# Stick-breaking layer of a two-block transformer kernel: query, key and gate products with the weights as the stationary operand, so that they and the outputs come out with features on the partitions

## The chip, the cores and the metric

The kernel runs on one core of a Trainium2 chip. The metric is the device time of one execution in microseconds, the median of several runs; lower is better. Everything is fp32 in memory, one sequence of 256 rows, width 2048.

## The reference

Two blocks follow each other. The second block has two layers: one with indexed sparse attention, then the stick-breaking layer that is changed here. Each layer ends in a layer norm and a gated per-layer embedding. The part that matters:

```python
def _stick_breaking_mixer(x, k, v, w_q, w_out):
    q, g = _split(x @ w_q, (ATTN_W, ATTN_W))                  # gate g, queries q: 16 heads of 128
    def block(args):                                          # blocks of 128 query rows
        i, qb = args
        t = i * B_BLOCK + jnp.arange(B_BLOCK)
        z = jnp.einsum('bqhd,bshd->bhqs', qb, k) * scale
        strict = (key_pos[None, :] < t[:, None])[None, None]
        log_keep = jnp.where(strict, jax.nn.log_sigmoid(-z), 0.0)
        between = lax.cumsum(log_keep, axis=3, reverse=True) - log_keep
        a = jnp.where(strict, jnp.exp(jax.nn.log_sigmoid(z) + between), 0.0)
        o = jnp.einsum('bhqs,bshd->bqhd', a.astype(v.dtype), v)
        return o.reshape(B, B_BLOCK, ATTN_W)
    ...
    return (o * jax.nn.silu(g)) @ w_out

kb, vb = _split(x @ w_kv_b, (ATTN_W, ATTN_W))                 # in second_block, before that mixer
x = _layer_norm(DN_ALPHA * x + y, ln_g[i], ln_b[i])           # behind each mixer
x = x + (p[i] @ w_ple[i]) * jax.nn.sigmoid(x @ w_ple_gate[i])
```

So each of the 16 heads has queries q, keys k and values v of 256 rows by 128; scores z, a reverse running sum of their logarithms along the keys, an exponential, the product with v, the gate, and the output product. x is what the layer before left.

## The kernel before

**One stream of weights.** All weights lie packed in the order of use. A block of it is a *slot*: 128 partitions by 1024 values, two of the sixteen tiles of the contraction by 512 output columns. There are 800 slots, counted from 1 here. SyncE loads them into five raw buffers. ScalarE rounds a slot to fp32r (`whi`, line 1164), VectorE takes the difference (`wlo`, line 1511), and PE multiplies with three products instead of one: hi rows by hi weights, hi by lo, lo by hi (lines 849, 850, 851; the rows are `XH` and `XL`). There are three pairs of whi and wlo, so ScalarE may round slot n only when PE has done slot n - 3. PE takes a slot in twelve matmuls, with 128 columns of the rows as the stationary operand and 512 columns of weights moving; the result is 128 rows by 512 features in one PSUM bank for each half of the 256 rows, after eight slots. Such a product over all sixteen tiles is called a run here (`bq1` is the second run of queries); banks G0 to G3 serve runs in pairs, in turn.

**The layer.** Its slots are 606 to 733, in four groups c = 0 to 3 of four heads: runs bg (gate), bq, bk, bv, eight slots each; the output product ob follows from 734. ScalarE moves finished runs out of PSUM (`move_rows`, line 1221): bg through SiLU into `Gd`, bv into `Va`, bq and bk into a row buffer `nat`. Queries and keys are needed with features on the partitions, so the jobs `bq0` to `bk3` (kind "copy") turn each in 8 transposes on PE (line 860), and ScalarE and VectorE copy one bank each into `qTa` and `kTa`.

**The attention of a group** is the job st0 to st3, cut in steps: 0 scores on PE (line 911); 1 mask on VectorE, absolute value on ScalarE; 2 Exp; 3 Ln and a Relu; 4, 5, 6 running sums and subtraction on VectorE (lines 1818 and 1820), one for each third of the scores, with a Relu on ScalarE in 4 and 5; 7 Exp (line 1350); 8 the twelve tiles of weights turned on PE and copied out; 9 weights times values (line 953); 10 times gate on VectorE, line 1832; 11 the result turned back, 8 transposes, and copied into `FT`, from where jobs r4 split it into XH and XL for the output product.

**What sets the order.** A walk over the slots gives every engine its program: before slot s, the rounding and the difference of slot s + 2 (`takes`); the slot; the steps that the table BEHIND names for it; then, if a run ends, the `move` of it; then those of AFTER. Each engine executes its part in this order and waits on semaphores: `half_done` and `slot_done` from PE, `moved` of a bank from whoever emptied it, `hi_done` and `lo_done` for the weights. BEHIND has bq0.0 at slot 622, bk0.0 at 630, st0 from 638 to 650, st1 at 670 (step 0), 671 (1, 2), 672 (3), 673 (4), 675 (5), 676 (6), 678 (7), 679 (8), 680 (9), 681 (10, 11); st2 is 32 slots later, st3 runs from 730 to 743. ScalarE loads a table before a function that the loaded one does not hold; those loads are instructions of its queue.

## Time and profile before

| | us |
|---|---|
| median of 3 runs (2360.76 to 2361.06) | 2360.78 |
| profiled execution, its time | 2361.13 |
| its span, first to last instruction | 2359.8 |
| PE busy | 2345.6 |
| VectorE busy | 1466.2 |
| ScalarE busy | 1146.1 |
| window of the layer's first four groups, slots 606 to 733 | 383.37 |

The window is 1776.95 to 2160.32 us from the start of the span. The busy time of PE is a union of records whose ends are modelled; for its pace the distance from start to start is the thing to read. A record's duration of 0.39 us for a matmul that is followed by the next after 0.23 us is such an overlap. On ScalarE and VectorE, too, the next instruction may begin up to 0.1 us before the end of the last. DVE in a row is VectorE, ACT is ScalarE, PEld the loading of the stationary operand. A wait in a row of the timeline stands in brackets: how long the engine was idle before it and what released it.

### The profile page before, as it was taken

Reading aid. Unit: us, or ns where it says so; the run is one execution under the profiler, and the core shown is the slowest. Engines: PE = TensorE matmul, PEld = TensorE weight load, DVE = VectorE, ACT = ScalarE, POOL = GpSimd, SP = SyncE. Lnnn points to the kernel's source line nnn. Section 1 sums busy time; section 2 is a strip of 40 time slices with the busy share of each in tenths; the row PEclk is TensorE's granted clock in tenths of the full one; section 3 lists DMA queues with packets and bytes.
Section 4 is the critical chain, followed back from the end, with each engine's and each line's share of the span. In section 5 each row is a group of like instructions: output and inputs, shape, how many; then the busy total and the mean of one; then the engine's idle time right before and its main releaser. Section 6 shows DMA issues by size and latency. Waiting matters only on the chain.

```text
span 2359.8 us, 28659 instructions
## 1 busy us (share of the span) xinstructions
PE 2345.6 (99%) x11224; PEld 1956.8 (83%) x11224; DVE 1466.2 (62%) x2045; ACT 1146.1 (49%) x1483; POOL 39.6 (2%) x60
## 2 busy tenths in 40 slices
PE   9999999999999999999999999999999999999999
PEld 5688898988889888888888878888788888888877
DVE  7888765555546455776756775666765455456575
ACT  4344554544445554443344445454545556456453
POOL 0000000000000000000000000000200000000020
PEclk9999999999999999999999999999999999999999
DMA  9986643555554457887655655455665555555565
GB/s 396 396 308 206 198 148 117 178 173 189 190 167 140 142 176 254 293 289 248 214 193 185 196 180 168 153 170 187 229 209 188 176 180 169 179 168 172 198 221 177
DMA packets 131240, 478.97 MB, mean 203 GB/s; under 512 B 15281, under 2 KB 15537, under 8 KB 125985
## 3 DMA queue, kind: packets, MB, share of 16 engines
q1 hardware_dynamic: 126080, 458.41, 58.0%
q0 software_dynamic: 3728, 17.76, 2.0%
q8 instruction: 89, 1.46, 0.3%
q10 hardware_dynamic: 1298, 0.97, 0.1%
q14 instruction: 45, 0.37, 0.0%
HBM read 470.80 MB, written 6.29 MB: 202 GB/s over the span
## 4 chain that ended last, share of the span: by engine, by line
PE 94%; DVE 2%; DMA 2%; ACT 1%; issue 1%; SPq 0%; ACTq 0%; DVEq 0%
PE G L849 26%; PE G L851 26%; PE G L850 26%; PE A L860 4%; DMA ada<-in_weights 2%; PE A L849 2%; PE A L850 2%; PE A L851 2%; PE A L953 1%; PE G L845 1%; PE A L1025 1%; PE A L1008 1%; PE A L911 1%; DVE ada L1525 1%; DVE wlo L1511 1%
## 5 line engine op out<-in xcount | busy, mean ns | idle before, releaser
L1511 DVE TENSOR_TENSOR wlo<-raw,whi 128x1024 fp32r<-128x1024 f32 (+3 forms) x781 | 920.8, 1183 | 696.8 <-ACT whi L1164 694.6
L1164 ACT ACTIVATE whi<-raw 128x1024 fp32r<-128x1024 f32 (+3 forms) x781 | 800.4, 1026 | 823.3 <-PE G L851 735.3
L849 PE MATMUL G<-whi,XH 128*128 128x512 f32 (+3 forms) x2804 | 1081.0, 386 | 2.8 <-DVE wlo L1511 2.3
L851 PE MATMUL G<-whi,XL 128*128 128x512 f32 (+3 forms) x2804 | 1066.9, 381 | 0.0
L850 PE MATMUL G<-wlo,XH 128*128 128x512 f32 (+3 forms) x2804 | 1066.0, 380 | 0.0
L849 PEld LDWEIGHTS G<-whi,XH 128*128 128x128 f32 x2804 | 526.7, 188 | 100.3 <-DVE wlo L1511 7.0
L851 PEld LDWEIGHTS G<-whi,XL 128*128 128x128 f32 x2804 | 526.3, 188 | 94.4
L850 PEld LDWEIGHTS G<-wlo,XH 128*128 128x128 f32 x2804 | 526.9, 188 | 90.4 <-issue 0.2
L849 PE MATMUL A<-whi,XH 128*128 128x512 f32 x192 | 77.4, 403 | 1.6 <-DVE wlo L1511 1.6
L1525 DVE CUSTOM_DVE_ANT_0 ada<-ada,dil 128x2048 f32<-128x2048 f32 x32 | 75.1, 2347 | 5.3 <-DMA ada<-in_weights 5.3
L850 PE MATMUL A<-wlo,XH 128*128 128x512 f32 x192 | 74.8, 390 | 0.0
L851 PE MATMUL A<-whi,XL 128*128 128x512 f32 x192 | 74.8, 389 | 0.0
L1221 ACT ACTIVATE nat<-G 128x512 f32<-128x512 f32 (+3 forms) x98 | 54.1, 569 | 29.3 <-PE G L851 29.1
L1221 ACT ACTIVATE dil<-G 128x512 f32<-128x512 f32 x64 | 36.8, 597 | 24.6 <-PE G L851 24.5
L849 PEld LDWEIGHTS A<-whi,XH 128*128 128x128 f32 x192 | 36.0, 188 | 12.6 <-issue 2.7
L1543 DVE SCALAR_TENSOR_TENSOR accg<-raw,small,accg 128x512 f32<-128x512 f32 x60 | 44.9, 748 | 1.1
L850 PEld LDWEIGHTS A<-wlo,XH 128*128 128x128 f32 x192 | 36.1, 188 | 8.4 <-issue 1.2
L851 PEld LDWEIGHTS A<-whi,XL 128*128 128x128 f32 x192 | 36.0, 188 | 7.6
L860 PE MATMUL A<-ident,nat 128*128 128x128 f32 x306 | 41.0, 273 | 0.5 <-ACT PT__91 L1295 0.5
L860 PEld LDWEIGHTS A<-ident,nat 128*128 128x128 f32 x306 | 35.8, 140 | 6.5 <-issue 0.9
L1288 ACT ACTIVATE dil<-A 128x512 f32<-128x512 f32 x25 | 14.9, 597 | 49.2 <-PE A L860 49.2
L1300 ACT ACTIVATE FT<-A 128x512 f32<-128x512 f32 x12 | 7.2, 597 | 51.8 <-PE A L860 51.8
(235 smaller groups left out, 1516.0 us busy)
## 6 DMA issues: line engine op xcount, KB each, us to landing
raw<-in_weights SPq DMA_DIRECT2D x724, 512.0 KB, 3.8
ada<-in_weights SPq DMA_DIRECT2D x32, 1024.0 KB, 11.2
raw<-in_weights SPq DMA_DIRECT2D x80, 384.0 KB, 3.2
raw<-in_weights SPq DMA_DIRECT2D x16, 288.0 KB, 2.9
spill<-nat POOLq DMA_DIRECT2D x8, 512.0 KB, 5.4
CP<-spill POOLq DMA_DIRECT2D x8, 512.0 KB, 6.3
raw<-in_weights SPq DMA_DIRECT2D x8, 336.0 KB, 3.5
FT<-in_xT SPq DMA_DIRECT2D x4, 512.0 KB, 5.8
```

The lines of the kernel that those rows point to most:

```text
L845: ins = pe.matmul(acc, whole_operand(name)[:, k, half], raw[o.home[n]][:, w], start=(k == start), stop=(k == end - 1))
L849: pe.matmul(acc, xh[:, k, half], wh, start=(k == start), stop=False)
L850: pe.matmul(acc, xh[:, k, half], wl, start=False, stop=False)
L851: ins = pe.matmul(acc, xl[:, k, half], wh, start=False, stop=(k == end - 1))
L860: ins = pe.transpose(P[bank][0:a.shape[1], 128 * n:128 * n + 128], a, ident[:, :])
L911: ins = pe.matmul(P[bank][:, x:x + nk], l, r, start=(n == 0), stop=(n == len(ps) - 1))
L953: ins = pe.matmul(P[A0 + qb][:, h * 128:(h + 1) * 128], PT[:, n * 128:(n + 1) * 128], v(h, kb), start=(kb == 0), stop=(kb == qb))
L1164: ac.activation(whi[r % NSPL][:, 0:2 * cols], raw[o.home[n]][:, 0:2 * cols], ACT.Copy).then_inc(hi_done, 1)
L1221: ac.activation(dst[:, hf, 0:cols], P[bank][:, 0:cols], func).then_inc(moved[bank], 1)
L1511: ve.tensor_tensor(wlo[r % NSPL][:, 0:2 * cols], raw[o.home[n]][:, 0:2 * cols], whi[r % NSPL][:, 0:2 * cols].bitcast(F32), ALU.subtract).t ...
L1525: ve.tensor_tensor_reduce(b, b, cs, 1.0, cols_[:, f:f + 1], ALU.mult, ALU.add, mods[:, f:f + 1]).then_inc(modulated, 1)
L1543: ins = ve.scalar_tensor_tensor(out=dst, in0=b, scalar=cc, in1=dst, op0=ALU.mult, op1=ALU.add)
```

## The change

The products bg, bq and bk of the layer take the weights as the stationary operand and the rows as the moving one, so the result has features on the partitions.

- Each of these twelve runs becomes two, `a` and `b`, of 256 output columns (two heads) and four slots. A slot now holds four contraction tiles by 256 columns. The count of slots stays 800.
- XH and XL become the two halves of one tensor `XHL`, tile by tile, so that one matmul moves 512 columns, XH and XL of a tile, past a tile of whi; a second moves XH alone, 256 columns, past wlo. A slot is sixteen matmuls (`turned_slot`): two heads by four contraction tiles by two. The bank then holds hi and lo parts side by side.
- When a run ends, VectorE adds the two parts of each head with a reduction (`TENSOR_REDUCE`, 128x512 to 128x256) directly into its place in `qTa`, `kTa` or the gate. For bg, ScalarE then applies SiLU in place, waiting for both reductions. ScalarE no longer moves bg, bq and bk out of PSUM.
- The jobs bq and bk (transposes and copies) are gone. Step 9 multiplies the values, as stationary operand, with the turned weights, 4 matmuls of 256 and 4 of 128 columns in fp32; the outputs come out turned. Step 10 multiplies by the turned gate and writes FT; step 11 is gone.
- In group 0, bv0 is placed ahead of bg0; in the other groups the order stays.

```diff
+    def plan_turned(w, c0):
+        for half in range(2):
+            plan.extend(("w", w, c0 + 256 * half, 512, k) for k in range(0, KT, 4))
+
     for c in range(4):
-        plan_gemm([("w_qb", 2048 + 512 * c, 512, KT), ("w_qb", 512 * c, 512, KT),
-                   ("w_kvb", 512 * c, 512, KT), ("w_kvb", 2048 + 512 * c, 512, KT)])
+        if c == 0:
+            plan_gemm([("w_kvb", 2048, 512, KT)])
+        plan_turned("w_qb_t", 2048 + 512 * c)
+        plan_turned("w_qb_t", 512 * c)
+        plan_turned("w_kvb_t", 512 * c)
+        if c:
+            plan_gemm([("w_kvb", 2048 + 512 * c, 512, KT)])
...
-        return {0: (A0, A1, A3), 8: (A2, A1, A3), 9: (A0, A1), 11: (A2, A3)}.get(step, ())
+        return {0: (A0, A1, A3), 8: (A2, A1, A3), 9: (A0, A1)}.get(step, ())
...
-        for x in "gqkv":
-            whole_run(f"b{x}{c}")
+        if c == 0:
+            whole_run("bv0")
+        for x in "gqk":
+            for half in "ab":
+                run(f"b{x}{c}{half}", 512, "T")
+                slots.extend((f"b{x}{c}{half}", k) for k in range(0, KT, 4))
+        if c:
+            whole_run(f"bv{c}")
...
-    XH = sb("XH", 53376, [128, KT, T], F32R)
-    XL = sb("XL", 69760, [128, KT, T], F32R)
+    XHL = sb("XHL", 53376, [128, KT, 2, T], F32R)
+    XH, XL = XHL[:, :, 0, :], XHL[:, :, 1, :]
...
+    GT = [g.rearrange("p q n -> p (q n)").rearrange("p (h t) -> p h t", h=4) for g in Gd]
...
+    def turned_place(name):
+
+        dst = {"q": qTa, "k": kTa, "g": GT[int(name[2]) % 2]}[name[1]]
+        return dst[:, 0:2, :] if name[3] == "a" else dst[:, 2:4, :]
...
-            elif name in ("om0", "oa0", "bg0", "ob0"):
-                job = {"om0": "r1", "oa0": "r2", "bg0": "r3", "ob0": "r4"}[name]
+            elif name in ("om0", "oa0", "bv0", "ob0"):
+                job = {"om0": "r1", "oa0": "r2", "bv0": "r3", "ob0": "r4"}[name]
...
+        def turned_slot(s):
+
+            name, k0 = slots[s]
+            if k0 == 0:
+                for bank, nth in use[name]:
+                    pe.wait_ge(moved[bank], nth - 1)
+            pe.wait_ge(lo_done, o.rank[s] + 1)
+            wh, wl = whi[o.rank[s] % NSPL], wlo[o.rank[s] % NSPL]
+            for h in range(2):
+                acc = P[use[name][h][0]]
+                for kk in range(4):
+                    k = k0 + kk
+                    w = slice(256 * kk + 128 * h, 256 * kk + 128 * h + 128)
+                    both = XHL[:, k, :, :].rearrange("p s t -> p (s t)")
+                    if k < KT - 1:
+                        pe.matmul(acc[:, :], wh[:, w], both, start=(k == 0), stop=False)
+                        ins = pe.matmul(acc[:, 0:T], wl[:, w], XH[:, k, :], start=False, stop=False)
+                    else:
+                        pe.matmul(acc[:, 0:T], wl[:, w], XH[:, k, :], start=False, stop=False)
+                        ins = pe.matmul(acc[:, :], wh[:, w], both, start=False, stop=True)
+                if h == 0 and k0 + 4 == KT:
+                    ins.then_inc(half_done, 1)
+            ins.then_inc(slot_done, 1)
...
-                weighted_values(job, step, PT2, lambda h, kb: Va[:, kb, h * 128:(h + 1) * 128])
-            elif step == 11:
-                heads_turned(job, step, S2, 9)
+                for bank, nth, _ in fill[(job, 8)]:
+                    pe.wait_ge(moved[bank], nth)
+                for bank, nth, _ in fill[(job, 9)]:
+                    pe.wait_ge(moved[bank], nth - 1)
+                for h in range(4):
+                    acc = P[(A0, A1)[h // 2]][:, h % 2 * T:h % 2 * T + T]
+                    v = [Va[:, kb, h * 128:(h + 1) * 128] for kb in range(2)]
+                    pe.matmul(acc, v[0], PT2[:, 384 * h:384 * h + 256], start=True, stop=False)
+                    ins = pe.matmul(acc[:, 128:256], v[1], PT2[:, 384 * h + 256:384 * h + 384], start=False, stop=True)
+                    if h % 2:
+                        ins.then_inc(side_full, 1)
...
-            elif name in ("bg2", "bg3"):
-                bank, nth, _ = fill[(f"st{int(name[2]) - 2}", 9)][1]
-                ac.wait_ge(moved[bank], nth)
...
-            elif name[:2] in ("ag", "bg"):
+            elif name[:2] == "ag":
                 gate_room(name)
                 move_rows(name, Gd[int(name[2]) % 2], ACT.Silu)
+            elif name[:2] == "bg":
+                for bank, nth in use[name]:
+                    ac.wait_ge(moved[bank], nth)
+                ac.activation(turned_place(name), turned_place(name), ACT.Silu).then_inc(gate_made, 1)
...
+            elif name[:2] in ("bg", "bq", "bk"):
+                turned_room(name)
+                for h in range(2):
+                    product_done(name, h)
+                    bank = use[name][h][0]
+                    ve.tensor_reduce(turned_place(name)[:, h, :], P[bank][:, :].rearrange("p (s t) -> p t s", s=2),
+                                     AX, ALU.add).then_inc(moved[bank], 1)
...
+        def turned_room(name):
+
+            c = int(name[2])
+            if name[1] != "g":
+                ve.wait_ge(side_full, fill[(f"st{c - 1}" if c else "att3", 0)][2][2])
+            elif c == 0:
+                ve.wait_ge(ple_added, 8)
+            else:
+                for bank, nth, _ in fill[(f"st{c - 2}", 9) if c > 1 else ("att3", 5)]:
+                    ve.wait_ge(moved[bank], nth)
...
-                rows = S2[:, 0:1024].rearrange("p (q n) -> p q n", q=2)
-                for bank, nth in use[f"bg{c}"]:
-                    ve.wait_ge(moved[bank], nth)
-                for qb in range(2):
-                    bank, nth, no = fill[(job, 9)][qb]
+                ve.wait_ge(gate_made, 2 * c + 2)
+                for n in range(2):
+                    bank, nth, no = fill[(job, 9)][n]
                     ve.wait_ge(side_full, no)
-                    ve.tensor_tensor(rows[:, qb, :], P[bank][:, :], Gd[c % 2][:, qb, :], ALU.mult).then_inc(moved[bank], 1)
-            elif step == 11:
-                heads_moved(job, step, 4 * c)
+                    ve.tensor_tensor(FT[:, 4 * c + 2 * n:4 * c + 2 * n + 2, :], P[bank][:, :].rearrange("p (h t) -> p h t", h=2),
+                                     GT[c % 2][:, 2 * n:2 * n + 2, :], ALU.mult).then_inc(moved[bank], 1)
```

Three places where the order of instructions moves. First PE in bk3: the end of its first slot (718), the turning of bq3 and the start of the next slot (nat is the row buffer, ident the identity; A is one of the banks A0 to A3, G one of G0 to G3). Before:

```order
L851 MATMUL G<-whi_56,XL 128x512
L849 MATMUL G<-whi_56,XH 128x512
L850 MATMUL G<-wlo_59,XH 128x512
L851 MATMUL G<-whi_56,XL 128x512
L860 MATMUL A<-ident,nat_70 128x128 x8
L849 MATMUL G<-whi_54,XH 128x512
L850 MATMUL G<-wlo_57,XH 128x512
L851 MATMUL G<-whi_54,XL 128x512
```

After, PE in a turned slot of the same group, in bq3a (in these rows the moving operand is named first):

```order
L906 MATMUL G<-XHL,whi_54 128x512
L907 MATMUL G<-XHL,wlo_57 128x256
L906 MATMUL G<-XHL,whi_54 128x512
L907 MATMUL G<-XHL,wlo_57 128x256
L906 MATMUL G<-XHL,whi_54 128x512
L907 MATMUL G<-XHL,wlo_57 128x256
```

The transposes are gone there, and matmuls of 512 and 256 columns alternate.

Second, VectorE beside st1, from the difference for slot 675 (wlo_58) on; L1818 are the four running sums of step 4 (TENSOR_TENSOR_SCAN in the trace), L1820 their subtraction. Before:

```order
L1511 TENSOR_TENSOR wlo_58<-raw_51,whi_55 128x1024
L1818 SCALAR_TENSOR_TENSOR CP<-dil,CP 128x128 x4
L1820 TENSOR_TENSOR dil<-dil,CP 128x512
L1511 TENSOR_TENSOR wlo_59<-raw_52,whi_56 128x1024
L1511 TENSOR_TENSOR wlo_57<-raw_53,whi_54 128x1024
L1818 SCALAR_TENSOR_TENSOR CP<-dil,CP 128x256 x2
L1820 TENSOR_TENSOR dil<-dil,CP 128x512
```

After, where L1905 and L1907 are the same two lines and L1725 the two reductions of bg2a:

```order
L1580 TENSOR_TENSOR wlo_58<-raw_51,whi_55 128x1024
L1905 SCALAR_TENSOR_TENSOR CP<-dil,CP 128x128 x4
L1907 TENSOR_TENSOR dil<-dil,CP 128x512
L1725 TENSOR_REDUCE dil<-G 128x256 x2
L1580 TENSOR_TENSOR wlo_59<-raw_52,whi_56 128x1024
L1580 TENSOR_TENSOR wlo_57<-raw_53,whi_54 128x1024
L1905 SCALAR_TENSOR_TENSOR CP<-dil,CP 128x256 x2
```

The reductions stand between the subtraction and the differences for slots 676 and 677.

Third, ScalarE at the same place; L1344 is the Ln of step 3, L1345 and L1347 Relu, whi_56 and whi_54 the rounding of slots 676 and 677. Before:

```order
L1344 ACT_TABLE_LOAD
L1344 ACTIVATE dil<-dil,ones 128x512 x3
L1345 ACTIVATE CP<-dil 128x512
L1164 ACTIVATE whi_55<-raw_51 128x1024
L1347 ACTIVATE CP<-dil 128x512
L1164 ACTIVATE whi_56<-raw_52 128x1024
L1164 ACTIVATE whi_54<-raw_53 128x1024
L1347 ACTIVATE CP<-dil 128x512
L1164 ACTIVATE whi_55<-raw_49 128x1024
L1164 ACTIVATE whi_56<-raw_50 128x1024
L1221 ACT_TABLE_LOAD
L1221 ACTIVATE dil<-G 128x512 x2
```

After, with L1415, L1416 and L1418 for those lines and L1331 the SiLU of bg2a, then of bg2b:

```order
L1415 ACT_TABLE_LOAD
L1415 ACTIVATE dil<-dil,ones 128x512 x3
L1416 ACTIVATE CP<-dil 128x512
L1239 ACTIVATE whi_55<-raw_51 128x1024
L1418 ACTIVATE CP<-dil 128x512
L1331 ACT_TABLE_LOAD
L1331 ACTIVATE dil<-dil 128x512
L1239 ACTIVATE whi_56<-raw_52 128x1024
L1239 ACTIVATE whi_54<-raw_53 128x1024
L1418 ACTIVATE CP<-dil 128x512
L1239 ACTIVATE whi_55<-raw_49 128x1024
L1239 ACTIVATE whi_56<-raw_50 128x1024
```

The SiLU and its table load stand ahead of the rounding of slots 676 and 677; before, they stood behind the rounding of 679.

## Rows read from the trace of the kernel before

**Rows 1.** the page: busy time of PE (section 1), the chain by engine (section 4)
```profile
PE 2345.6 (99%) x11224; PEld 1956.8 (83%) x11224; DVE 1466.2 (62%) x2045; ACT 1146.1 (49%) x1483; POOL 39.6 (2%) x60
...
PE 94%; DVE 2%; DMA 2%; ACT 1%; issue 1%; SPq 0%; ACTq 0%; DVEq 0%
```

**Rows 2.** windows, slots 638 to 669: length; busy PE, PEld, DVE, ACT, POOL; clock; DMA
```profile
1866.70:1963.42 96.72, 96.72 (x461) 80.86 (x460) 50.15 (x52) 53.77 (x62) 0.00 (x0) 1.00 0.54 174
```

**Rows 3.** timeline of PE: start, duration; fp32r matmuls of 288 and 512 columns
```profile
243.77 0.29 PE L850 MATMUL G<-wlo,XH 128*128 128x288 f32 x1
...
244.83 0.29 PE L849 MATMUL G<-whi,XH 128*128 128x288 f32 x1
...
1988.46 0.39 PE L849 MATMUL G<-whi,XH 128*128 128x512 f32 x1
...
1991.18 0.39 PE L849 MATMUL G<-whi,XH 128*128 128x512 f32 x1
```

**Rows 4.** timeline of PE: slots 622 and 623, with the turning of bq0
```profile
1821.36 0.39 PE L849 MATMUL G<-whi,XH 128*128 128x512 f32 x1
...
1824.09 1.04 PE L860 MATMUL A<-ident,nat 128*128 128x128 f32 x8
1824.88 0.47 PE L849 MATMUL G<-whi,XH 128*128 128x512 f32 x1
...
1827.73 0.39 PE L849 MATMUL G<-whi,XH 128*128 128x512 f32 x1
```

**Rows 5.** timeline of PE: scores of st0, then its values and turned outputs
```profile
1869.42 2.78 PE L911 MATMUL A<-dil 128*128 128x128 f32 x16
1871.86 0.58 PE L849 MATMUL G<-whi,XH 128*128 128x512 f32 x1
...
1903.62 2.84 PE L953 MATMUL A<-dil,CP 128*128 128x128 f32 x24
1906.21 0.48 PE L849 MATMUL G<-whi,XH 128*128 128x512 f32 x1
...
1909.83 0.48 PE L849 MATMUL G<-whi,XH 128*128 128x512 f32 x1
...
1912.64 0.39 PE L849 MATMUL G<-whi,XH 128*128 128x512 f32 x1
```

**Rows 6.** groups by line and shape: reductions on VectorE; busy us, mean ns
```profile
L1770 DVE TENSOR_REDUCE st__92<-S__90 128x1 f32<-128x768 f32 x8 | 7.5, 942 | 0.0
...
L1769 DVE TENSOR_REDUCE st__92<-S__90 128x1 f32<-128x384 f32 x8 | 4.4, 553 | 0.3
```

**Rows 7.** timeline of ScalarE beside st1: start, duration, idle before
```profile
1973.71 1.28 ACT L1344 ACT_TABLE_LOAD   x1
...
1977.38 1.05 ACT L1164 ACTIVATE whi<-raw 128x1024 fp32r<-128x1024 f32 x1
1978.33 0.62 ACT L1347 ACTIVATE CP<-dil 128x512 f32<-128x512 f32 x1
1978.85 2.12 ACT L1164 ACTIVATE whi<-raw 128x1024 fp32r<-128x1024 f32 x2
...
1991.98 1.49 ACT L1350 ACTIVATE dil<-dil 128x1536 f32<-128x1536 f32 x1
```

**Rows 8.** timeline of VectorE beside st1
```profile
1978.46 1.23 DVE L1511 TENSOR_TENSOR wlo<-raw,whi 128x1024 fp32r<-128x1024 f32 x1 [3.51 <-ACT whi L1164]
1979.60 1.36 DVE L1818 TENSOR_TENSOR_SCAN CP<-dil,CP 128x128 f32<-128x128 f32 x4
1981.00 0.69 DVE L1820 TENSOR_TENSOR dil<-dil,CP 128x512 f32<-128x512 f32 x1
1981.61 2.35 DVE L1511 TENSOR_TENSOR wlo<-raw,whi 128x1024 fp32r<-128x1024 f32 x2
```

**Rows 9.** timeline of PE: first matmuls of slots 675 and 676
```profile
1979.74 0.50 PE L849 MATMUL G<-whi,XH 128*128 128x512 f32 x1
...
1982.88 0.50 PE L849 MATMUL G<-whi,XH 128*128 128x512 f32 x1
```

65 lines of the change are left out of this document (37 added, 28 removed), and 13 rows, old and new, of the table BEHIND.

## The prediction

> **What bounds the kernel now.** The page comes first. Matmuls fill 2345.6 of the 2359.8 us, and 94% of the chain of waits is on PE [rows 1], so a saving counts only if it takes time out of PE's own row of work, and a wait counts only if PE meets it. The windows by stretch say the same of the layer that is changed: its second group of heads, from 1866.70 to 1963.42, has PE busy in all 96.72 us at a granted clock of 1.00, while VectorE works 50.15 and ScalarE 53.77 us [rows 2]. Both look half idle. But every slot of weights passes through both in turn (the rounding on ScalarE, line 1164, then the difference on VectorE, line 1511), only three slots of room ahead of PE, and both engines take their instructions in a fixed order. So the timelines of ScalarE and VectorE beside the attention steps must be read, not their busy shares.
>
> A slot is twelve matmuls of 512 columns. From its first start to that of the next slot lie 2.72 us (1988.46 to 1991.18), 0.227 a matmul. With 288 columns eight steps take 1.06 us (243.77 to 244.83), 0.133 each [rows 3]. The durations in the rows (0.39 and 0.29) overlap; only starts count here.
>
> **What leaves PE.** (1) The turning of query and key rows: 8 transposes behind one slot for each of the eight tiles bq and bk. The slot that starts at 1821.36 is followed at 1824.88, 3.52 us on where 2.72 would be undisturbed, and the next slot takes 2.85 until 1827.73 [rows 4]. That is 0.80 + 0.13, about 0.9 us for each of eight: 7.3 us. (2) The turning of the outputs, step 11 of the four st jobs: the same 8 transposes, slots at 1906.21, 1909.83 and 1912.64 [rows 5]. 3.62 + 2.81 against 5.44 is 1.0, of which about 0.1 belongs to the step before: 0.9 each, 3.7 us in all. (3) Weights times values: 24 records of 128 columns take 2.59 us (1903.62 to 1906.21 [rows 5]). Now there are 8 of 256 and 8 of 128, the shape of today's scores, whose 16 records take 2.44 (1869.42 to 1871.86 [rows 5]): 0.15 less, 0.5 us over four. Sum: -11.5 us. The ScalarE and VectorE copies that go with (1) and (2) are off the path and give nothing by themselves. Twenty-four ScalarE moves out of PSUM also go; that frees ScalarE where it already waits for PE.
>
> **What comes onto PE.** The 96 slots of bg, bq and bk keep their 6144 columns but spread them over sixteen matmuls: eight of 512 and eight of 256, each with its own weight load. No fp32r matmul of 256 columns is in the trace. A line through the two steps of [rows 3] (0.227 at 512, 0.133 at 288, so 0.42 ns a column and 12 ns a matmul) gives 0.120 us at 256. A slot then takes 8 x 0.227 + 8 x 0.120 = 2.775 us, 0.053 more: +5.1 us over 96. The bounds: below, 0.108 us, the step of the 24 records of values, each with its load (2.59 / 24 [rows 5]); above, the 0.133 of the 288 columns, which would hold if the load and not the columns set that step. Over 768 short matmuls that is -9 to +10 us. I take 0.120 because 288 columns, the nearest row, still follow the line. The Trainium skill, TensorE: Matmul & The Clock Gate, section Back-to-back issue gap, gives columns / 2.4 + 2.5 ns for a matmul; by it the extra four matmuls would cost 0.01 us a slot, 1 us in all instead of 5, but it also gives 216 ns for 512 columns where this trace has 227, so the rows stand.
>
> **What is moved: the reductions and the gate.** Every turned tile now ends with two reductions on VectorE (hi part plus lo part, 128x512 from PSUM to 128x256). The reductions in the trace take 553 ns for 384 elements and 942 for 768 [rows 6], 1.0 ns an element, so 0.68 us for 512; the next instruction starts about 0.08 earlier, so 0.60 each. For bq and bk that hides: rounding and difference (1.06 and 1.23 us [rows 7, 8]) have two slots of 2.72 to be done in, so 1.2 us of reductions fit into what is left. For the gate it does not, because ScalarE's SiLU, which used to read PSUM on its own, now waits in ScalarE's queue for VectorE's second reduction, and the rounding of the next slots stands behind it. And bg is now two tiles of four slots, so the first gate tile ends at slot 673, in the middle of the scans of st1, where before the only gate move came at slot 677.
>
> I work st1 through on the clock of before. VectorE: the difference for slot 675 starts at 1978.46, four scans at 1979.60, their subtraction at 1981.00, and it is free at 1981.61 [rows 8]. There the differences for slots 676 and 677 stand now, and PE starts slot 676 at 1982.88 [rows 9]. In the changed order the two reductions come first: free at 1982.8, result out at 1982.9. ScalarE has been waiting for that since 1978.9; before it had rounded slot 676 from 1978.85 on [rows 7]. Now the table load for SiLU (1.28 us, as the one at 1973.71 [rows 7]), 0.5 us of SiLU (a ScalarE step of 512 at 1978.33 hands on after 0.52 [rows 7]), and the rounding of 676 starts at 1984.7 instead of 1978.85. Rounding to difference is 1.1 us (1977.38 to 1978.46), the difference 1.23: slot 676 can start at 1987.1. PE starts slot 675 at 1979.74 [rows 9] and is through at 1982.5. **PE waits about 4.4 us.** Behind that the two other scan steps of st1 are late too: difference 676, 677, scans and subtraction of step 5 (1.9), difference 678, step 6 (1.9), difference 679, the two reductions of the second gate tile, at 1995.4; then SiLU (0.5), a rounding (0.95), the table load for Exp (1.28) and the Exp (1.49 [rows 7]) end at 1999.9, while PE stands before step 8 from 1998.2: 1.7 us more. So st1 costs 6.1, where the same slots lose 0.64 today (0.42 of it at 1982.88 [rows 9] and the rest as small waits at slots 674 and 676). Net +5.4. The steps of st2 stand at the same slots relative to theirs: +5.4. For st0 the first gate tile ends one slot earlier in its scans (slot 641, with step 4 at 642), so the reductions run before the scans and only table load and SiLU delay the rounding, by 1.9 us, of which slack takes some: 1.6 us; the second gate tile comes behind step 6 and holds the rounding of 648 until PE has lost 1.8 more. 3.4 against 0.3 today: +3.1. st3 has no gate tile beside it: 0. Sum of new waits: +13.9 us. Bounds: if a reduction takes 0.55 instead of 0.68 the waits are 1.4 us less, at 0.9 (a strided read of PSUM, which no row shows) 2 us more.
>
> bv0 moves ahead of bg0; it waits for the same x_lo counts, and its values now lie ready early. One more wait is new on PE, that step 0 waits for reductions in place of copies; for st0 the last of them ends about 0.9 us behind slot 637 and PE has slot 638 in between, so nothing.
>
> **The sum.** -11.5 + 5.1 + 13.9 = +7.5 us. The chains above pass some ten times from engine to engine, which I took at nothing and which costs about 0.05 us each time (1977.38 + 1.05 against 1978.46 [rows 7, 8]): +8.0 us. The profiled execution has a span of 2359.8 [rows 1] and a time of 2361.13, so it becomes 2367.8 and 2369.1; its time is 0.35 above the median of 2360.78, and the forecast for the median is 2368.8 us, 0.34% slower. A measurement of this kernel can tell about 0.2% (4.7 us) from no change.
>
> **Rivals.**
> *The gate queue doesn't bind (faster).* If the table load is over before the reductions end, or ScalarE and VectorE run ahead further than I have them because their copies are gone, the waits stay what they are and -11.5 + 5.1 = -6.4: 2354.4 us. For it: both engines are half idle [rows 2]. Against: the wait comes from order, not load, and the slack of slot 676 is 1.7 us (its rounding starts at 1978.85, with 2.4 of work, for a use at 1982.88 [rows 7, 9]). The rival holds if the rounding of 676 starts before about 1980.5 on this clock. Chance 0.13, with half of it spread between this and no change.
> *The short matmul is bound by its weight load.* 0.133 us instead of 0.120, +10 us, of which the waits give 3 back: 2376. For it: each matmul has its load and none so short is in the trace. Against: 288 columns and the 128-column transposes [rows 3, 4]. Chance 0.11.
> *A 256-column fp32r matmul runs at the fp32 rate.* The scores' rows [rows 5] are 8 of 256 and 8 of 128 columns in 2.44 us, about 0.2 us for each of 256: 768 x 0.09 = +70 us, 2438. Nothing in the trace speaks for it. Chance 0.02.
> *PE's clock falls in the pause.* The granted clock is 1.00 in all of the layer [rows 2], but PE is busy in all of it, and here two pauses of over 4 us come. At 1.2 GHz a turned slot takes twice its 2.78 us; one slot at that level in each of two places is +5.6 us, less what the later wait of 1.7 takes back: about 2373. The Trainium skill, TensorE: Matmul & The Clock Gate, section Part 1: The HAM clock gate, says that an idle engine falls to half its clock; no run here shows at what pause. Chance 0.10.
>
> **How the numbers follow.** The forecast has 0.62, with its own range from 2363 (short matmul near its lower bound) to 2375 (slower reductions). The rest is as above, 0.02 unnamed. To hold 8 in 10 the range reaches to the clock case and over most of the load case and part of the way to the faster one: 2358 to 2379. Slower by over 0.2% (above 2365.5): 0.52 of the forecast, 0.10, 0.11 and 0.02 make 0.75. Faster (below 2356.1): 0.09 of the first rival and 0.01. Within: the remaining 0.15.
>
> **What would show it.** In the changed trace: no transposes of nat beside bq and bk, and none behind the values; turned slots 2.775 us apart, eight starts 0.120 and eight 0.227 us; reductions of 0.68 us; a ScalarE table load before each first gate SiLU that waited for VectorE; PE waiting for the difference (line 1511's successor) once for over 4 us in each of the second and third groups, at the third slot behind the first gate tile, and for the Exp before step 8; for 1 to 2 us twice in the first. The window of the second group should be 96.7 - 2.9 + 1.3 + 3.1 = 98.2 us, that of the third some 2.3 longer. I am wrong if the layer's slots are 2.72 or over 2.83 us, or if the rounding of the third slot doesn't stand behind the SiLU.

## The result, and the profile after

The changed kernel takes 2375.44 us (median of 4 runs, 2374.29 to 2376.70), the kernel before 2360.92 beside it (4 runs, 2360.76 to 2362.83): slower by 0.6%, ratio 1.006 [1.0042, 1.0077]. The forecast was 2368.8, range 2358 to 2379. The sign, the place and the main mechanism came as written. The time is 6.6 us above the forecast, though. For the profiled execution, forecast at 2369.1, it is 5.2: the turned slots are slower by 4.3 than forecast, two more terms that were off by nearly 4 each, TensorE's clock and the waits, cancel, and the time outside the span adds 1.4, less 0.7 that was gained ahead of the layer.

The profiled execution took 2374.29 us with a span of 2371.6 (before 2361.13 and 2359.8 [rows 1]): +11.8 in the span and 1.4 outside it. The page, sections 1 and 4, which answer to [rows 1]:

```profile
PE 2346.3 (99%) x11480; PEld 1968.2 (83%) x11480; DVE 1487.1 (63%) x2081; ACT 1131.2 (48%) x1455; POOL 39.6 (2%) x60
...
PE 92%; DVE 3%; DMA 2%; ACT 2%; issue 1%; SPq 0%; ACTq 0%; DVEq 0%
```

PE is hardly busier than before (2346.3 against 2345.6), so what left it and what came onto it, slots at a lower clock included, nearly cancel. The span grew by what PE stood still, and VectorE and ScalarE together have 2 points more of the chain. The windows by stretch say where: the kernel before first (slots 614 to 637, 670 to 701, 702 to 729, 730 to 765; 638 to 669 is [rows 2]), then the changed kernel (the same stretches, with 638 to 669 second). The columns are those of [rows 2]; the clock is third from the end.

```profile
1799.60:1866.70 67.10, 67.10 (x305) 55.72 (x304) 30.79 (x26) 30.32 (x34) 0.00 (x0) 1.00 0.58 188
1963.42:2060.54 97.12, 96.99 (x462) 80.77 (x460) 50.23 (x52) 52.48 (x61) 0.00 (x0) 1.00 0.53 173
2060.54:2146.81 86.27, 86.14 (x413) 71.77 (x412) 47.10 (x51) 49.21 (x59) 0.00 (x0) 1.00 0.52 170
2146.81:2250.87 104.06, 103.42 (x481) 85.86 (x480) 62.33 (x70) 52.86 (x60) 0.53 (x1) 1.00 0.57 188
```

```profile
1798.88:1866.71 67.83, 67.83 (x385) 58.84 (x384) 35.56 (x35) 28.16 (x28) 0.00 (x0) 1.00 0.55 186
1866.71:1965.97 99.26, 96.57 (x526) 82.82 (x524) 56.18 (x63) 49.61 (x54) 0.00 (x0) 1.00 0.51 170
1965.97:2067.93 101.96, 97.72 (x525) 84.12 (x524) 55.63 (x61) 48.70 (x54) 0.00 (x0) 0.98 0.47 165
2067.93:2159.59 91.66, 87.42 (x477) 75.66 (x476) 52.57 (x60) 45.44 (x52) 0.00 (x0) 0.96 0.46 160
...
2159.59:2262.67 103.08, 102.44 (x465) 84.80 (x464) 61.63 (x69) 52.38 (x59) 0.53 (x1) 1.00 0.56 190
```

The five differences are +0.73, +2.54, +4.84, +5.39 and -0.98 us, +12.5 together (the first 605 slots happened to be 0.7 quicker). The second stretch holds the scans of st0, the third those of st1, the fourth those of st2; where the forecast and the expectations speak of waits in the first, second and third group, these are meant. The stretches with st0 and st1 were forecast at 98.2 and 100.5 us and are 99.26 and 101.96. Those with st1 and st2 lose most, and they alone show a clock below 1.00.

**The queue behind the gate.** ScalarE beside st1, the place of [rows 7]; then VectorE, the place of [rows 8]; then PE at slots 676 and 677 and at 708 and 709, the place of [rows 9]:

```profile
1980.96 0.62 ACT L1418 ACTIVATE CP<-dil 128x512 f32<-128x512 f32 x1
1985.60 1.28 ACT L1331 ACT_TABLE_LOAD   x1 [4.02 <-DVE dil L1725]
1986.89 0.63 ACT L1331 ACTIVATE dil<-dil 128x512 f32<-128x512 f32 x1
1987.43 1.99 ACT L1239 ACTIVATE whi<-raw 128x1024 fp32r<-128x1024 f32 x2
```

```profile
1981.09 1.23 DVE L1580 TENSOR_TENSOR wlo<-raw,whi 128x1024 fp32r<-128x1024 f32 x1 [3.51 <-ACT whi L1239]
1982.23 1.36 DVE L1905 TENSOR_TENSOR_SCAN CP<-dil,CP 128x128 f32<-128x128 f32 x4
1983.63 0.69 DVE L1907 TENSOR_TENSOR dil<-dil,CP 128x512 f32<-128x512 f32 x1
1984.24 1.28 DVE L1725 TENSOR_REDUCE dil<-G 128x256 f32<-128x512 f32 x2
1988.50 2.36 DVE L1580 TENSOR_TENSOR wlo<-raw,whi 128x1024 fp32r<-128x1024 f32 x2 [2.98 <-ACT whi L1239]
```

```profile
1989.78 0.50 PE L906 MATMUL G<-XHL,whi 128*128 128x512 f32 x1 [4.24 <-DVE wlo L1580]
...
1994.24 0.39 PE L906 MATMUL G<-XHL,whi 128*128 128x512 f32 x1
...
2091.75 0.80 PE L906 MATMUL G<-XHL,whi 128*128 128x512 f32 x1 [4.24 <-DVE wlo L1580]
...
2096.78 0.40 PE L906 MATMUL G<-XHL,whi 128*128 128x512 f32 x1
```

Read them as one chain. ScalarE is done with its Relu at 1981.6 and stands for 4.02 us before the gate's SiLU, because VectorE has a difference, four scans and a subtraction to do before the two reductions. These end at 1985.5, and only then do the table load, the SiLU and the rounding follow (1987.43), the difference (1988.50), and PE, which had slot 675 done 4.24 us earlier. Slot 676 then takes 4.46 us (1989.78 to 1994.24) and slot 708 takes 5.03, where an undisturbed turned slot takes 2.83. The granted clock over them, from the windows:

```profile
1989.78:1994.24 4.46, 4.46 (x17) 3.83 (x18) 4.43 (x6) 1.10 (x2) 0.00 (x0) 0.62 0.67 229
2091.75:2096.78 5.03, 5.03 (x17) 4.31 (x17) 5.00 (x7) 1.10 (x2) 0.00 (x0) 0.53 0.59 208
```

TensorE was at its lower level, 1.2 GHz, for most of both: that cost 1.6 and 2.2 us at these two slots. Beside st0 PE waits 1.15 and 1.50 us (idle times ahead of its first matmuls at 1887.44 and 1900.81), and the clock stays up.

**The turned slots.** PE's timeline, starts of one slot in the quicker and one in the slower rhythm that they show:

```profile
1874.93 0.39 PE L906 MATMUL G<-XHL,whi 128*128 128x512 f32 x1
...
1877.70 0.39 PE L906 MATMUL G<-XHL,whi 128*128 128x512 f32 x1
...
1927.23 0.40 PE L906 MATMUL G<-XHL,whi 128*128 128x512 f32 x1
1927.47 0.28 PE L907 MATMUL G<-XHL,wlo 128*128 128x256 f32 x1
1927.58 0.40 PE L906 MATMUL G<-XHL,whi 128*128 128x512 f32 x1
...
1930.07 0.40 PE L906 MATMUL G<-XHL,whi 128*128 128x512 f32 x1
```

2.77 us from slot start to slot start in the first, as forecast; 2.83 in the second, and that is the usual one: of the 96 turned slots only some ten, behind a step 0 or a step 9, are quick. In the turned slots of the trace a long matmul is followed by a short one after 0.235 us (median) and a short one by a long one after 0.117.

### The profile page after: what moved, and what is told of

It is laid out like the page before. It is cut to its first block, busy times and chain, and to the rows that moved or that the text cites. A ratio compares the mean times of both kernels' runs of the same rounds, so it can differ in the third digit from the quotient of the medians.

```text
span 2371.6 us, 29207 instructions
## 1 busy us (share of the span) xinstructions
PE 2346.3 (99%) x11480; PEld 1968.2 (83%) x11480; DVE 1487.1 (63%) x2081; ACT 1131.2 (48%) x1455; POOL 39.6 (2%) x60
## 4 chain that ended last, share of the span: by engine, by line
PE 92%; DVE 3%; DMA 2%; ACT 2%; issue 1%; SPq 0%; ACTq 0%; DVEq 0%
PE G L884 23%; PE G L886 23%; PE G L885 23%; PE G L906 6%; PE A L919 3%; PE G L907 3%; DMA ada<-in_weights 2%; PE A L884 2%; PE A L885 2%; PE A L886 2%; PE G L880 1%; PE A L1018 1%; DVE wlo L1580 1%; PE A L1098 1%; PE A L1081 1%
## 5 line engine op out<-in xcount | busy, mean ns | idle before, releaser
L884 PE MATMUL G<-whi,XHL 128*128 128x512 f32 (+3 forms) x2420 | 928.9, 384 | 2.2 <-DVE wlo L1580 2.0
L886 PE MATMUL G<-whi,XHL 128*128 128x512 f32 (+3 forms) x2420 | 917.3, 379 | 0.0
L885 PE MATMUL G<-wlo,XHL 128*128 128x512 f32 (+3 forms) x2420 | 916.6, 379 | 0.0
L884 PEld LDWEIGHTS G<-whi,XHL 128*128 128x128 f32 x2420 | 454.6, 188 | 83.2 <-DVE wlo L1580 4.4
L886 PEld LDWEIGHTS G<-whi,XHL 128*128 128x128 f32 x2420 | 454.3, 188 | 79.4
L885 PEld LDWEIGHTS G<-wlo,XHL 128*128 128x128 f32 x2420 | 454.9, 188 | 76.0 <-issue 0.2
L906 PE MATMUL G<-XHL,whi 128*128 128x512 f32 x720 | 261.1, 404 | 11.2 <-DVE wlo L1580 11.1
L907 PE MATMUL G<-XHL,wlo 128*128 128x256 f32 x720 | 203.5, 283 | 0.0
L906 PEld LDWEIGHTS G<-XHL,whi 128*128 128x128 f32 x720 | 137.1, 190 | 43.8 <-DVE wlo L1580 12.8
L907 PEld LDWEIGHTS G<-XHL,wlo 128*128 128x128 f32 x720 | 137.8, 191 | 2.3
L884 PE MATMUL A<-whi,XHL 128*128 128x512 f32 x192 | 77.2, 402 | 1.6 <-DVE wlo L1580 1.6
L885 PE MATMUL A<-wlo,XHL 128*128 128x512 f32 x192 | 74.8, 389 | 0.0
L886 PE MATMUL A<-whi,XHL 128*128 128x512 f32 x192 | 74.7, 389 | 0.0
L884 PEld LDWEIGHTS A<-whi,XHL 128*128 128x128 f32 x192 | 36.1, 188 | 11.8 <-issue 2.7
```

What stands on the lines that cost most here:

```text
L884: pe.matmul(acc, xh[:, k, half], wh, start=(k == start), stop=False)
L885: pe.matmul(acc, xh[:, k, half], wl, start=False, stop=False)
L886: ins = pe.matmul(acc, xl[:, k, half], wh, start=False, stop=(k == end - 1))
L906: pe.matmul(acc[:, :], wh[:, w], both, start=(k == 0), stop=False)
L907: ins = pe.matmul(acc[:, 0:T], wl[:, w], XH[:, k, :], start=False, stop=False)
```

## The experiments

All times are medians. The kernel before took 2360.6 to 2360.8 us beside every one of them.

**The SiLU out of the scans.**

```diff
-            elif name[:2] == "bg":
-                for bank, nth in use[name]:
-                    ac.wait_ge(moved[bank], nth)
-                ac.activation(turned_place(name), turned_place(name), ACT.Silu).then_inc(gate_made, 1)
+            elif name[:2] == "bk" and name[3] == "b":
+                for gate in (f"bg{name[2]}a", f"bg{name[2]}b"):
+                    for bank, nth in use[gate]:
+                        ac.wait_ge(moved[bank], nth)
+                    ac.activation(turned_place(gate), turned_place(gate), ACT.Silu).then_inc(gate_made, 1)
```

> The changed kernel with the two gate SiLUs of each group taken out of the scans and done behind the last key tile of the group. Theory (ScalarE's queue stands behind the gate's reduction): the rounding for slot 676 runs at once, only the 1.2 us of reductions still stand before its difference, so PE waits 1.3 us there instead of 4.4, the same in the third group, the waits of the first group (1.3, 1.7 and some tenths) go, and TensorE's clock stays at 1.00, which gives back 1.7 and 2.2 us: 2375.4 - 6.2 - 3.5 - 3.9 = about 2362. Rival (VectorE's reductions make the wait, and the queue only adds the 1.9 us of table load and SiLU to it): PE still waits over 2 us in each group, about 2369. Rival (the time is in the slots, not in the waits): within 1 us of the changed kernel.

Measured: 2364.22 us, ratio to before 1.0015 [1.0006, 1.0024]; clock 1.00 in every stretch of the layer. Moving two short instructions on an engine that is half idle gives 11.2 of the 14.5 us back. The wait behind slot 675 is 1.5 us (1.3 expected), so the theory holds and both rivals fall. By the profiled spans (2371.6 and 2362.2) the gain is 9.4 us, though, where the theory has 13.6. Of what is missing, 3.5 us stand in waits that were in no trace so far: 1.24 us each at slots 674 and 706, 1.04 at slot 735.

**The reduction out of the scans too.** In the walk, behind the slot and ahead of its steps:

```diff
+            late = self.slots[s - 2]
+            if late[0][:2] == "bg" and late[0][3] == "a" and late[1] == 12:
+                self.walk.append(("move", late[0], 0))
```

> As the kernel with the late SiLUs, and the reductions of each group's first gate tile two slots later, behind the difference for slot 677. Theory: no new wait is left beside the scans; what remains of the change is 11.5 us of PE work removed and 96 slots of 2.83 in place of 2.72 us (+10.3): 2360.9 - 11.5 + 10.3 = about 2359.7, and clock 1.00. If the reductions cost the same wherever they stand (rival): as the kernel with the late SiLUs alone, about 2362.

Measured: 2363.00 us, 1.001 [1.0, 1.002], against 2359.7 expected. The wait behind slot 675 is down to 0.3 us as expected, but the new waits at 674, 706 and 735 stay, and the stretch with st0 is now 0.9 us longer (96.68 against 95.77 us by the windows): there the reduction had been in a free place. ScalarE's timeline beside step 2 of st1 in this kernel shows where the new wait comes from:

```profile
1971.94 1.28 ACT L1416 ACT_TABLE_LOAD   x1
1973.23 1.67 ACT L1416 ACTIVATE dil<-dil 128x512 f32<-128x512 f32 x3
```

The groups of ScalarE's instructions by line count the loads ahead of this Exp, first in the kernel before (line 1340), then in this one:

```profile
L1340 ACT ACT_TABLE_LOAD x1 | 1.3, 1283 | 0.0
```

```profile
L1416 ACT ACT_TABLE_LOAD x4 | 5.1, 1283 | 0.1
```

One in the whole layer before, one in each group now. With the SiLU behind bk the last Exp's table is gone when step 2 comes, and the 1.28 us fall into ScalarE's busiest stretch. In the kernel before, and in the changed one, SiLU stood between Ln and Exp. It took a load of its own there too, but the Exp behind it needed one in any case. The traces count 41 loads in each of these two kernels, 44 with the late SiLUs, and 37 where a copy stands in place of SiLU (below).

**The table loaded early.** `bg1a` is reduced in its old place, and behind the late SiLUs:

```diff
+                ac.activation(spare[:, 0:1], ident[:, 0:1], ACT.Exp)
```

> As the kernel with both late, with two mends: the first gate tile of the first group is reduced where it was (there the later place cost 0.9 us: 96.67 against 95.77 us for that group), and behind the two late SiLUs stands an Exp of one column, so that ScalarE loads the table for Exp where it has time. Theory (the new waits of the late kernels, 1.24 us at slots 674 and 706 and 1.04 us at slot 735, are one more table load of 1.28 us that came to stand at step 2 of the scans): 2363.0 - 0.9 - 2.5 - 1.0 = about 2358.6, and slot 674 takes 2.81 us. Rival (the load hides in any place, the waits come from something else): 2362.

Measured: 2358.18 us, 0.9989 [0.998, 0.9998]. The waits at 674, 706 and 735 are gone (slot 674 takes 2.81 us, slot 735 3.41 as in the kernel before), and all of PE's time beside the scans is work. The windows, slots 614 to 729 in four stretches:

```profile
1799.59:1867.42 67.83, 67.83 (x386) 58.84 (x384) 35.68 (x35) 27.43 (x27) 0.00 (x0) 1.00 0.57 187
1867.42:1963.19 95.77, 95.77 (x525) 82.82 (x524) 56.08 (x63) 52.08 (x59) 0.00 (x0) 1.00 0.55 176
1963.19:2059.36 96.17, 96.17 (x525) 82.91 (x524) 55.47 (x61) 50.35 (x56) 0.00 (x0) 1.00 0.55 175
2059.36:2144.68 85.32, 85.32 (x477) 73.92 (x476) 52.14 (x60) 47.07 (x54) 0.00 (x0) 1.00 0.53 169
```

So the change as such is a small gain (about 2.5 us), which its queue order, with all that followed from it, had buried under 17.

**Query and key alone.** Gate, values and outputs as in the kernel before, with step 11 back in its places:

```diff
-        for x in "gqk":
+        whole_run(f"bg{c}")
+        for x in "qk":
             for half in "ab":
```

> One part of the change alone: query and key products turned, gate, values and the turning of the outputs as in the kernel before. Theory (only the gate's turning makes PE wait): -7.3 us for the 64 transposes and their trailing slots, +7.0 for 64 slots of 2.83 in place of 2.72, reductions of query and key hidden: 2360.8 - 0.3 = about 2360.5, with waits beside the scans as in the kernel before and clock 1.00. Rival (the reductions on VectorE or the slots of four tiles cost beside the scans by themselves): over 2363.

Measured: 2359.59 us, 0.9995 [0.9986, 1.0004]; clock 1.00, and no wait of PE that the kernel before does not have. The reductions of query and key cost nothing beside the scans; the whole loss comes with the rest of the change, and the kernels above put it on the gate.

**The pause filled.** Twelve matmuls that read only XHL, behind slots 675 and 707:

```diff
             ins.then_inc(slot_done, 1)
+            if s + 1 in (675, 707):
+                for _ in range(12):
+                    pe.matmul(acc[:, :], XH[:, 0, 0:128], both, start=False, stop=False)
```

> The changed kernel with twelve more matmuls of 512 columns (2.7 us) put on PE at the start of the pause of 4.4 us behind slots 675 and 707; they add to the gate's sums, so the output is not the reference's. Nothing else moves. Theory (the clock falls because PE stands still for over 4 us): the pauses are 1.7 us, the granted clock stays 1.00 behind them, the slots behind them take 2.8 instead of 4.5 and 5.0 us; the waits before step 8 of up to 1.7 us, which the slow slots hid, come back in part: 1 to 4 us less than the changed kernel, 2371.5 to 2374.5. Rival (the fall has another cause, such as the power of the short matmuls): the clock falls at the same places and the time stays within 1 us.

Measured: 2372.74 us, 1.0051 [1.0036, 1.0066], clock 1.000 in all four runs where the changed kernel had 0.996 to 0.998. PE's waits beside st1, and the window behind the first:

```profile
1989.70 0.50 PE L906 MATMUL G<-XHL,whi 128*128 128x512 f32 x1 [1.50 <-DVE wlo L1583]
...
2002.59 1.53 PE L922 MATMUL A<-ident,dil 128*128 128x128 f32 x12 [1.43 <-ACT dil L1424]
```

```profile
1989.70:1993.00 3.30, 3.30 (x19) 2.89 (x20) 3.27 (x5) 1.22 (x3) 0.00 (x0) 1.00 0.70 214
```

The same time passes, but PE is at work in it, and the clock stays. This shows that the pause makes the clock fall. It also shows the second wait of the forecast, the one before step 8 (1.7 us forecast, 1.43 here), which the changed kernel doesn't have: there the slow slots give the scans the time. So the clock's fall costs 3.8 us where it happens and much less in the end. In the profiled executions the stretch with st1 takes 101.96 us with the pause filled and without, and the one with st2 91.11 in place of 91.66: 0.6 us in all, because slots 679 and 711, behind which the wait stands, take 5.65 and 5.62 us to the next slot in place of 4.13 and 4.06. The median spans (2372.7 and 2371.1) differ by 1.6 and the median times by 2.7; what differs between the executions of the changed kernel is open. The low level does not last equally long in all: in the profiled one with the banks in turn (below), slot 676 took 5.12 us.

**A copy in place of SiLU.** One word, `ACT.Copy` for `ACT.Silu`; no table load in the chain.

> The changed kernel with a plain copy in place of the gate's SiLU, in the same place of ScalarE's order: no table load before it (1.28 us). The gate is left without its SiLU, so the output is not the reference's. Theory (reductions, table load and SiLU stand one behind the other ahead of the rounding): the pauses behind slots 675 and 707 shrink by the load alone, from 4.24 to 2.96 us, that in the first group from 1.15 to about 0, and TensorE's clock does not fall behind them, while the waits before step 8 grow to some 1.4 us as they did with the pause filled: 2375.4 - 2.6 - 1.1 - 3.9 + 2.6 = about 2370.4. Rival (a pause of 3 us is enough for the clock to fall): about 2372. Rival (the load is over before the reductions are): no change.

Measured: 2369.71 us, 1.0037 [1.0023, 1.0051]. The pauses and the clock of the slots behind them:

```profile
1986.80 0.80 PE L906 MATMUL G<-XHL,whi 128*128 128x512 f32 x1 [2.96 <-DVE wlo L1580]
...
2088.60 0.80 PE L906 MATMUL G<-XHL,whi 128*128 128x512 f32 x1 [2.96 <-DVE wlo L1580]
```

```profile
1986.80:1992.09 5.29, 5.29 (x16) 4.51 (x17) 5.25 (x7) 1.11 (x2) 0.00 (x0) 0.50 0.64 205
2088.60:2092.95 4.35, 4.35 (x16) 3.73 (x17) 4.32 (x6) 1.10 (x2) 0.00 (x0) 0.63 0.69 210
```

4.24 - 2.96 = 1.28 us, the table load to the hundredth: it is in the chain and nothing hides it. The Trainium skill, ScalarE: Activation LUTs, section What ACT_TABLE_LOAD costs, adds a drain of about 1.38 us to each load; here the measurement decides, and there is none: the SiLU starts at 1986.89, where the load that began at 1985.60 ends. The 2370.4 was near for a wrong reason, though: the clock was to stay up, and it fell after 2.96 us too. By the two profiled spans the kernel gains 3.7 us, 2.6 in the pauses and 1.4 in the stretch with st0 (97.83 against 99.26), while the slow slots cost 0.5 more (5.29 and 3.12 at slots 676 and 677 and 4.35 at slot 708, in place of 4.46, 2.81 and 5.03) and hide the wait before step 8 as they did. The median gains 5.7, since the other runs of the changed kernel have spans of 0.7 to 1.9 us more than its profiled one.

**The order of PE's matmuls.** Three orders of the same sixteen. Grouped, on the changed kernel:

```diff
-                for kk in range(4):
+                last = k0 + 4 == KT
+                for kk, long in [(kk, long) for long in ((False, True) if last else (True, False)) for kk in range(4)]:
```

Banks in turn, on the changed kernel: `for kk in range(4) for h in range(2)` in all slots but a tile's last. And, on the kernel with the early table, one order in all slots; in the changed kernel the last k-tile of a half has its short matmul ahead of its long one:

```diff
-                    if k < KT - 1:
...
-                    else:
-                        pe.matmul(acc[:, 0:T], wl[:, w], XH[:, k, :], start=False, stop=False)
-                        ins = pe.matmul(acc[:, :], wh[:, w], both, start=False, stop=True)
+                    pe.matmul(acc[:, :], wh[:, w], both, start=(k == 0), stop=False)
+                    ins = pe.matmul(acc[:, 0:T], wl[:, w], XH[:, k, :], start=False, stop=(k == KT - 1))
```

> The changed kernel with the matmuls of each half slot in another order: four of 512 columns, then four of 256 (the last slot of a tile the other way round), instead of in turn. The measured slot is 2.83 us, where eight steps of 0.227 and eight of 0.120 would be 2.775. Theory (the surplus of 0.055 comes from the alternation of long and short): slot 2.775, about 5 us less than the changed kernel, 2370. Rival (a short matmul behind a short one is bound by its weight load, 0.133 us): slot 2.88, about 5 us more, 2380. Rival (the surplus belongs to sixteen matmuls in whatever order): 2.83 and no change.

Measured: 2373.81 us, so neither the 2370 of the theory nor the 2380 of the first rival; a turned slot takes 2.80, and the first 24 take 67.32 us instead of 67.83. Short behind short starts after 0.119 us (median), so the load rival is out and the short step is the 0.120 of the line through [rows 3]. Long behind long starts after 0.234, where [rows 3] has 0.227. The surplus is in the long ones.

> The changed kernel with the two PSUM banks of a turned tile filled in turn, a pair of matmuls each, instead of eight matmuls into one and then eight into the other (the last slot of a tile stays as it is). What the grouped order showed: the short step is 0.120 us as worked out, the long one 0.234 instead of 0.227. Theory (a long matmul pays 7 ns because it adds to the bank that the one ahead of it wrote): turned slots of 2.775 us, 4 us less than the changed kernel, about 2371.5. Rival (the bank has nothing to do with it): 2.83, no change, 2375.4.

Measured: 2373.87 us (2372.56 to 2375.26); turned slots 2.83 as in the changed kernel, and the steps are the same 0.235 and 0.117. So the slots don't depend on the bank; the theory falls. The 1.6 us between the medians are not in the slots, and the times of two of the four runs (2375.06 and 2375.26) lie among those of the changed kernel.

> As the kernel with the table loaded early, but the last k-tile of a turned half keeps the order of all others (512 columns, then 256); there it was the other way round, so two long and two short matmuls stood side by side. In the traces so far a turned slot takes 2.773 us behind the scores or values of a step and 2.83 from the next tile's first slot on. Theory (the turned-round pair at a tile's end takes PE out of the quicker rhythm): the slots behind each step 0 and step 9 stay at 2.77 until the next disturbance, so up to 2 us less, 2356.5. Rival (the rhythm has another cause): no change, 2358.2.

Measured: 2356.53 us, 0.998 [0.9971, 0.9989]. From step 0 of st0 on the undisturbed turned slots take 2.77 us, all but 709 to 711, behind a short wait, with 2.83. One of group 1 by its starts:

```profile
1918.02 0.39 PE L910 MATMUL G<-XHL,whi 128*128 128x512 f32 x1
1918.25 0.28 PE L911 MATMUL G<-XHL,wlo 128*128 128x256 f32 x1
1918.37 0.39 PE L910 MATMUL G<-XHL,whi 128*128 128x512 f32 x1
...
1920.79 0.39 PE L910 MATMUL G<-XHL,whi 128*128 128x512 f32 x1
```

The 24 slots ahead of step 0 still take 67.83 us. A long matmul is followed after 0.236 us there (median) and after 0.230 in a quick slot. So the odd pair at a tile's end takes PE out of the quick rhythm, but it is not the only thing that does, and something in the attention steps brings PE in.

> As the grouped kernel with late SiLUs, but every slot has its four long matmuls ahead of its four short ones, in the last slot of a tile too. Theory as above (the turned-round order at a tile's end sets the rhythm): turned slots of 2.78 in place of 2.805 us, up to 2 us less, 2355. Rival: no change, 2356.9.

Measured: 2357.01 us (2356.91 in the grouped order with the odd tile end, below): no change, 2.80 as before. The theory falls here: grouped slots have one rhythm, between the two.

The grouped order on the kernel with the early table:

> As the kernel with the table loaded early, with the grouped order of matmuls in the turned slots as well. Theory: the two gains add, since one is in waits and the other in PE's own steps (24 undisturbed turned slots took 67.33 instead of 67.83 us, 0.02 each): 2358.6 - 2.0 = about 2356.6, under the kernel before by 0.18%. Rival (shorter slots let PE reach the same waits earlier, and they take it back): 2358.6.

Measured: 2356.91 us, 0.9984 [0.9975, 0.9992]: 1.3 of the 2.0 us.

```diff
+            if s + 1 == 614:
+                for _ in range(4):
+                    pe.matmul(P[use[name][0][0]][:, 0:128], ident[:, :], ident[:, :], start=True, stop=True)
```

> As the kernel with one order in all turned slots, with four fp32 products of the identity with itself (128 columns) put on PE ahead of the first turned slot, 614; their sums are overwritten by the tile's first matmul. The 24 turned slots ahead of the first attention step still took 2.83 us there, all behind it 2.77. Theory (any few short fp32 matmuls ahead of a turned tile put PE into the quicker rhythm, which then lasts): these 24 take 2.773, so 1.37 us less and 0.45 for the four, 2356.5 - 0.9 = 2355.6, and the stretch of slots 614 to 637 takes 67.0 instead of 67.83 us. Rival (the rhythm comes from something else in the attention steps, such as the wait for another engine): the stretch takes 67.83 + 0.45 = 68.3 us, 2357.0.

Measured: 2355.86 us, 0.9978 [0.9969, 0.9987], the lowest median of all and 0.22% under the kernel before. The slots behind the four are at 2.77 us until the scores of st0; the slots 640 to 648 behind these scores are at 2.83, where they were at 2.77 without the four (starts of PE, slots 622 and 623 and then 641 and 642, and the window from slot 614 to the scores of st0, ahead of it that of the kernel without the four):

```profile
1821.56 0.39 PE L913 MATMUL G<-XHL,whi 128*128 128x512 f32 x1
...
1824.34 0.39 PE L913 MATMUL G<-XHL,whi 128*128 128x512 f32 x1
...
1876.98 0.40 PE L913 MATMUL G<-XHL,whi 128*128 128x512 f32 x1
...
1879.81 0.40 PE L913 MATMUL G<-XHL,whi 128*128 128x512 f32 x1
```

```profile
1799.21:1869.86 70.65, 70.65 (x401) 61.31 (x400) 36.61 (x36) 30.22 (x31) 0.00 (x0) 1.00 0.54 186
```

```profile
1798.48:1868.71 70.23, 70.23 (x409) 62.02 (x408) 36.60 (x36) 30.12 (x31) 0.00 (x0) 1.00 0.54 187
```

The four themselves took 0.81 us (1798.48 to 1799.29), not 0.45, so 0.4 is left in that stretch where 0.9 was expected. The stretch with st0 gives it back (95.45 in place of 94.97 us), so the 0.7 us between this median and the one of the kernel with one order is not shown to come from the four. What is shown is that short fp32 matmuls change the step of what follows, and not only to the quicker one; why, and what decides between the two, no run here shows.

## Why the prediction was right, and by how much it was off

The sum of the prediction against the rows. The last column comes from the distances between slot starts in the two traces: for the 96 slots what the undisturbed ones take over 2.72 us (67.83 - 65.28 = 2.55 in the first stretch, 2.2 to 2.35 in each of the others), for waits and clock what the disturbed ones take over that:

| term | forecast, us | by the trace, us |
|---|---|---|
| transposes, values, turned outputs leave PE | -11.5 | -11.4 |
| 96 slots of sixteen matmuls | +5.1 | +9.4 |
| new waits, hand-overs included | +14.4 | +10.7 |
| TensorE's clock | 0 (rival) | +3.8 |
| sum over slots 606 to 765 | +8.0 | +12.5 |

**What leaves PE** was right: 1.8 us a group for query and key, 0.9 to 1.0 for step 11 and values.

**What comes onto PE** was mis-sized. The step that failed is not the one I had bounded. The short matmul is at 0.117 to 0.120 us, on the line through [rows 3]. The long one was taken over unchanged at 0.227, since it is the commonest row of the trace, and in its new surroundings it takes 0.235. Two bounds for the unknown form and none for the known one: the row's 0.227 holds among matmuls like it. The kernel with one order then had the slot of the forecast, 2.77, by steps of 0.230 and 0.117. This term is the one that failed: it was put at +5.1 us and measured +9.4, and these 4.3 us are nearly all of the 4.5 by which the sum over the slots is off.

**The waits** were right where the prediction had worked them out on the rows. Behind slot 675 PE waits 4.4 us by the slots' starts, 4.4 forecast; beside st0 3.2 more than before, 3.1 forecast. The reductions take 0.68 us each and ScalarE's table load waits for them, as forecast; the answer on their line (min, median, max, then who waited):

```profile
L1725 DVE TENSOR_REDUCE dil<-G x48: 677/682/692, 1809.8 to 2149.0; 128x256 f32<-128x512 f32 x48
...
  ACT L1331: 10.6, 3
```

Only the 1.7 us before step 8 of st1 and st2 are missing from the changed kernel (under 0.1 there), and the kernel with the filled pause has them, 1.5 and 1.6 by the slots' starts.

**The clock** was the rival with 0.10, and its mechanism came true beside that of the forecast. Its "one slot at that level in each of two places" and the later wait that takes something back are in the trace, with 3.8 us in place of 5.6. That the total lies no farther off is owed to this: the clock, at nothing in the sum, cost 3.8 us, and the two later waits that it hides, 3.4 in the sum, are gone. That the two cancel is luck as far as the sum goes, which had neither the one nor the end of the other in it; the rival had named both. It was mis-weighed, not unseen: that PE is busy in all of the layer before says nothing for a pause that the change itself makes, and the forecast had just worked out two of 4.4 us. The Trainium skill, TensorE: Matmul & The Clock Gate, Part 1: The HAM clock gate, has an idle engine fall to half its clock; the trace agrees, with a granted clock of 0.50 to 0.63 over the slots behind the pauses of 4.24 and 2.96 us. The forecast with this rival inside would have been 8.0 + 2.2 (5.6 less 3.4 for two later waits, of which the rival's 2373 took off only one) = about 2371, and with the slots' true size about 2375.

**Outside the span** the profiled execution of the changed kernel has 2.7 us where that before had 1.3. Over its four runs it is 2.2 to 3.3. Over the runs of the other kernels it is mostly 1.3 for the kernel before (2.5 at most), 1.3 or 1.4 for query and key alone, and 1.6 or 1.7 for those with the turned gate, with 2 to 3.3 now and then. That is a part of the 6.6 us which no experiment here explains.

## What to carry to other kernels

When an instruction is given a new producer, look at what stands behind it in its engine's queue, not at how busy that engine is: here a SiLU of 0.6 us held up the rounding that feeds PE, and putting it behind the busy stretch, with the next table loaded early and a reduction moved, turned 0.6% slower into 0.1% faster. Before moving a function on ScalarE, follow the tables: the cheap place is one where the function behind it needs a load anyway, or where one can be made in idle time. If the forecast itself contains a pause of PE of some microseconds, price the slots behind it at the lower clock, and take off the later waits that they hide. And a step time taken from a trace holds for matmuls among their like: give it bounds where its neighbours change.
